# Expert results stored to their tokens' rows by indirect transfers, fetched back by nine plain ones; branches around further tiles nested

## The chip, the cores and the metric

One core of one Trainium2 chip runs the whole program. The metric is device time in microseconds (us), the median of three runs for the kernel before. The five engines (TensorE as PE, VectorE as DVE, ScalarE as ACT, GpSimd as POOL, SyncE as SP) each run their own instruction stream and meet at semaphores. SP and ACT issue plain transfers on queues q1 and q10, POOL issues its transfers, plain and indirect, on q0. All queues share the core's 16 DMA engines.

## The reference, cut to what matters

One step of a one-layer decoder: 1024 prompt tokens and 32 sample tokens, 1056 in all, width 1024, float32. First comes a mixer (gated delta net, S5), then a mixture of experts, which this change is about:

```python
x = x + mixed
# _hier_moe(h = _rmsnorm(x, norm_ffn_w)): 4 groups of 8 experts
g_sel = argmax(softmax(tok @ w_rc))               # one group
top_w, top_i = top_k(softmax(fine of that group), 2)   # two experts in it
top_w = top_w / sum(top_w) * p_sel
hu = tok @ w_eu[e]; gate, up = hu[:256], hu[256:]
act = silu(gate) * up * top_w                     # per token and expert
out = sum over the token's two experts of act @ w_ed[e]
y = _rmsnorm(x + out, norm_final_w)               # y_prompt, y_sample
```

Each token has two results, one of each of its experts; the output row is the normalised sum of its x row and the two weighted results.

## The kernel before, in words

The mixer runs to about 972 us. Then the router stage takes the nine tiles of 128 tokens (the last has 32) in the order WORD: PE multiplies a tile by w_o and by the router's weights, DVE chooses experts and works out slots (`choose`, `places`), and POOL scatters the tile's normalised rows h2 to x_d, twice, by indirect transfer (L648). x_d has 96 rows for each of the 32 experts.

The expert stage runs 32 tiles of 96 rows (one for each expert), three tiles' rows in four strips of 32, so that four strips make a chunk of 128 rows; there are 24 chunks. Per tile: PE's up product (L1289, L1292), a transposition of the next chunk (L1226), the down product of the tile before (L1261, L1265), a transposition of the activations (L1303). SP loads the weights, 2 MB and 1 MB a tile, three buffers deep (`expert`, L2720 and L2723). POOL loads the chunks of x_d (L677) into two buffers xg. ACT and DVE copy down results into one of three buffers yo (L2488, L1976), and when a chunk is complete ACT stores it with one plain transfer to y_d, in the order of slots (`chunks_done`, L2493).

If an expert has more than 96 tokens, further tiles are needed. Their number is known only at run time, so `expert_tiles` gives every engine first the 32 tiles and then six `If`s, one for each group of four further tiles. In this profile no further tile runs: the transfers of expert weights number 32, and the six `If`s are passed over on every engine. `result_rows` works out for each token and choice the row of y_d with its result (ypos_i). For the further tiles POOL also writes token numbers into idx_d (`further_rows`, inside the first `If`).

The end takes the nine token tiles in the order ORDER (the tile of 32 first). POOL gathers each tile's two sets of result rows by indirect transfer, 18 in all (L693), at most five tiles ahead. Tiles with odd p are summed on PE (L1317 adds x1 through an identity product, L1321 the two weighted results, 12 products of 512 columns a tile); those with even p on DVE (L2027, L2028 in `combine`). ACT squares and sums (L2528) and takes the root (L2530), DVE scales (L2036, L2040 in `normed`), SP stores the tile (L2780). DVE's order is combine(0), normed(0), combine(2), normed(1), normed(2), combine(4) and so on.

Eight clears of rows of y_d with zeros (L2575, Z_PARTS) lie in the projection stage of the mixer, between 313 and 456 us; ACT and POOL wait for them before they begin with experts.

Of the kernel before, what the change touches and what calls it, by code (L numbers as in the profile page):

```python
# [11 lines left out]
I32 = mybir.dt.int32  # L12
ALU = mybir.AluOpType
# [32 lines left out]
NTILE = E + TGROUP * -(-((2 * NT + E * (RT - 1)) // RT - E) // TGROUP)  # L46
NCHUNK = NTILE * RT // 128
CONV_ROWS = 4 * 12
NBK = 3
# [22 lines left out]
def hybrid_step(nc, x_p, x_s, st_conv, st_delta, st_re, st_im, norm_mix, w_in, conv_w, a_log, dt_bias, head_norm,  # L72
# [4 lines left out]
    with ctx:  # L77
# [231 lines left out]
        ypos_i = ypos_i.rearrange("p (a b) -> p a b", a=2)  # L309
        tokf, desf, tilef, idx_n, o_te = small(TT_), small(EG), small(NTILE), small(128)[0:NCHUNK], small(NOV)  # L310
        assert off[0] <= ARENA, off[0]
# [138 lines left out]
        GDEPTH = 5  # L450
        s_yg5 = s_yg + s_h2d
        GATHERED = [0, 0, 0] + [32 * ((TT_ + 1 - b) // 2) for b in range(2)]
        s_hat = sem("s_hat")
# [109 lines left out]

        def chunks_done(i):

            return [c for c in sorted({slot_of(i, s)[0] for s in range(NSTRIP)}) if chunk_last_tile(c) == i]

        heads = [slice(64 * b, 64 * b + 64) for b in range(2)]

        X_PARTS, Z_PARTS = 4, 8  # L570
        EARLY = NWE
# [4 lines left out]
        def _(pool):  # L576
# [60 lines left out]
            pl(pool.iota(des_i[:], pattern=[[1, NTILE]], base=0, channel_multiplier=0))  # L637
            pl(pool.memset(idx_n[:], 0.0))
            pool.sem_inc(s_io, 1)
            pool.wait_ge(s_yz, 1 + 16 * (X_PARTS + Z_PARTS))  # L640
            for p, i in enumerate(WORD):
                n = rows(i)
                pool.wait_ge(s_h2, p + 1)
                pool.wait_ge(s_pos, p + 1)
                if p == TT_ - 1:
                    pool.wait_ge(s_xg[0], 16)
                for j in range(2):
                    pool.indirect_dma_start(x_d, bass.IndirectOffsetOnAxis(pos_i[0:n, j, i:i + 1], 0), h2[p % 2][0:n, :],  # L648
                                            None, bounds_check=E * RT - 1, oob_is_err=False).then_inc(s_h2d[p % 2], 16)
                if p == TT_ - 2:  # L650
                    for b in range(2):
                        pool.wait_ge(s_h2d[b], 32 * ((TT_ - b) // 2))
                    pool.dma_start(xg_first, x_d[0:128, :]).then_inc(s_xg[0], 16)

            for b in range(2):
                pool.wait_ge(s_h2d[b], 32 * ((TT_ + 1 - b) // 2))

            def further_rows():
                pool.wait_ge(s_zid, 16)
                for b in range(2):  # L660
                    pool.wait_ge(s_h2s[b], H2S[b] + 16 * ((TT_ + 1 - b) // 2))
                for i in range(TT_):
                    n = rows(i)
                    for j in range(2):
                        pool.indirect_dma_start(idx_d, bass.IndirectOffsetOnAxis(ypos_i[0:n, j, i:i + 1], 0),
                                                tokf[0:n, i:i + 1], None).then_inc(s_sct, 16)
                pool.wait_ge(s_idx, 1)

            def run(lo, hi):
                if lo == E:  # L670
                    further_rows()
                for c in range(slot_of(lo, 0)[0], slot_of(hi, 0)[0]):
                    if c >= 2:
# [4 lines left out]
                    elif lo >= E:  # L678
                        pool.indirect_dma_start(xg[c % 2], None, h2_d, bass.IndirectOffsetOnAxis(idx_i[:, c:c + 1], 0)
                                                ).then_inc(s_xg[c % 2], 16)  # L680
# [5 lines left out]
            for p, i in enumerate(ORDER):  # L686
                n = rows(i)
                if p >= GDEPTH and summed_by_pe(p - GDEPTH):
                    pool.wait_ge(s_job, N_JOBS + (p - GDEPTH) // 2 + 1)
                elif p >= GDEPTH:  # L690
                    pool.wait_ge(s_acc, (p - GDEPTH) // 2 + 1)
                for j in range(2):
                    pool.indirect_dma_start(yg[2 * i + j][0:n], None, y_d,  # L693
                                            bass.IndirectOffsetOnAxis(ypos_i[0:n, j, i:i + 1], 0)
                                            ).then_inc(s_yg5[p % GDEPTH], 16)

        @block.tensor
        def _(pe):
# [571 lines left out]
            def run(lo, hi):  # L1270
                if lo == E:
                    pe.wait_ge(s_idn, 16)
                    pe.transpose(bank6()[:, 0:NCHUNK], idx_n[:], ident[0:NCHUNK, 0:NCHUNK]).then_inc(s_6, 1)
# [5 lines left out]
                for i in range(lo, hi):  # L1279
# [33 lines left out]
            for p, i in enumerate(ORDER):  # L1313
                if not summed_by_pe(p):
                    continue
                for o in range(2):
                    pe.matmul(bank_sum(p)[:, o, :], ident, x1[:, i, 512 * o:512 * o + 512], start=True, stop=False)  # L1317
                pe.wait_ge(s_yg5[p % GDEPTH], GATHERED[p % GDEPTH] + 32 * (p // GDEPTH + 1))
                for j in range(2):
# [6 lines left out]
        def _(dve):  # L1326
# [464 lines left out]
            dve.wait_ge(s_io, 1)  # L1791
            link(dve.tensor_copy(tokf, tok_i[:]))
            link(dve.tensor_copy(tilef, des_i[:]))
# [186 lines left out]
            def run(lo, hi):  # L1980
                if lo == E:
                    read6(dve.tensor_copy(idx_i[:], bank6()[:, 0:NCHUNK]))
                    dve.sem_inc(s_idx, 1)
                for c in new_chunks(lo, lo):
                    gathered(c)
                for i in range(lo, hi):
# [27 lines left out]
                    dve.wait_ge(s_hat, i + 1)  # L2014
                    dve.sem_inc(s_6f, 1)
                down(hi - 1)

# [4 lines left out]
            def combine(p):  # L2022
                i = ORDER[p]
                n = rows(i)
                dve.wait_ge(s_yg5[p % GDEPTH], GATHERED[p % GDEPTH] + 32 * (p // GDEPTH + 1))
                o = x1[0:n, i, :]
# [23 lines left out]
        def _(act):  # L2050
# [431 lines left out]
            def down(i):  # L2482
# [29 lines left out]

            act.wait_ge(s_yz, 1 + 16 * (X_PARTS + Z_PARTS))
            expert_tiles(act, run)
# [19 lines left out]
        def _(sp):  # L2534
# [69 lines left out]
            for n in range(N_JOBS_S5, N_JOBS_QKV):  # L2604
                weights(n)
                if n == AB:
                    sp.dma_start(abp[:, 0:1], a_log.rearrange("a h -> h a")).then_inc(s_abp, 16)
                    sp.dma_start(abp[:, 1:2], dt_bias.rearrange("a h -> h a")).then_inc(s_abp, 16)
                if AB < n <= AB + Z_PARTS:
                    part = (NTILE - E) * RT // Z_PARTS  # L2610
                    first = RT * E + part * (n - AB - 1)
                    cleared(y_d[first:first + part], part)
                if n == AB + 3:
# [132 lines left out]
            sp.dma_start(h2_d[128 * t:128 * t + 128, :], h2[(TT_ - 1) % 2]).then_inc(s_h2s[(TT_ - 1) % 2], 16)  # L2746
            sp.wait_ge(s_io, 1)
            sp.dma_start(idx_d.rearrange("(t p) a -> t (p a)", p=128), idx_n[:]).then_inc(s_zid, 16)
            def expert(i):
# [15 lines left out]

            def run(lo, hi):
                if lo == E:
                    sp.wait_ge(s_sct, 16 * 2 * TT_)
# [45 lines left out]
```

## Time and profile before

| | |
|---|---|
| median of three runs | 1516.19 us (1514.94 to 1517.57) |
| the profiled execution | 1514.86 us, of it 1513.1 us span |
| busy: PE, DVE, ACT, POOL | 92%, 49%, 26%, 10% of the span |
| router stage | about 972 to 1137 us |
| expert stage | about 1137 to 1442 us |
| end | about 1442 to 1513 us |
| DMA | 262.54 MB, mean 174 GB/s over the span |

Times of the trace are us from the start of the span. Each engine's line gives busy time and, ahead of an instruction, how long its engine was idle and what released it. "issue" means that the profile shows nothing that it waited for. In the view of stretches a row gives each engine's busy time with the number of instructions, then the granted TensorE clock as a share of full speed, the busy share of the DMA engines and GB/s. Instruction queues (q8, q14) are the transfers that bring the engines' own instructions.

### The profile page before, as it was taken

To read this page: it belongs to the slowest core of one execution; us is meant where nothing else is said; L and a number is where in the kernel's file an instruction comes from. 1 tells how busy PE (TensorE), PEld (TensorE's weight loads), DVE (VectorE), ACT (ScalarE), POOL (GpSimd) and SP (SyncE) were. 2 spreads that over 40 slices of the span, in tenths; PEclk is the share of its full clock that TensorE was granted. 3 is DMA by queue.
4 is the path that set the end of the run, shared out by engine and by line. 5 is a ranking of instruction groups with operands and counts; after the bars stand their busy time and mean duration, and the time that the engine had idled before them with its cause. 6 is when DMAs were issued, how large, how long until landed. Compare 5 with 4: busy or idle time off the path is not lost.

```text
span 1513.1 us, 26998 instructions
## 1 busy us (share of the span) xinstructions
PE 1386.5 (92%) x11499; PEld 967.5 (64%) x11499; DVE 743.9 (49%) x1376; ACT 389.9 (26%) x707; POOL 147.5 (10%) x152
## 2 busy tenths in 40 slices
PE   7999999999999999999967899999978999999906
PEld 6667666666666656656767666765547888888802
DVE  4667695403425532689687344355553433222324
ACT  4211100114536553232213110011112333333312
POOL 1000010000001000045036000001111000000031
PEclk9998999999999999999989899999979999999958
DMA  5243684543522113233331425334348999999755
GB/s 170 82 102 57 188 239 134 134 122 103 140 62 62 44 44 99 53 99 119 92 136 32 157 69 187 108 131 155 112 154 326 420 425 426 426 425 425 304 183 195
DMA packets 190050, 262.54 MB, mean 174 GB/s; under 512 B 61219, under 2 KB 159889, under 8 KB 181465
## 3 DMA queue, kind: packets, MB, share of 16 engines
q1 hardware_dynamic: 164668, 200.39, 39.9%
q10 hardware_dynamic: 16988, 30.29, 5.4%
q0 software_dynamic: 8256, 29.89, 5.3%
q8 instruction: 103, 1.69, 0.5%
q14 instruction: 35, 0.28, 0.1%
HBM read 184.64 MB, written 75.90 MB: 172 GB/s over the span
## 4 chain that ended last, share of the span: by engine, by line
PE 75%; DVE 9%; DMA 5%; issue 5%; ACT 3%; POOL 2%; ACTq 0%; POOLq 0%; SPq 0%; DVEq 0%
PE P L730 28%; PE P L1103 8%; PE P L1292 6%; PE P L1190 5%; PE P L1261 4%; PE P L1289 3%; DMA arena<-in_w_expert_up_dram 2%; PE P L892 2%; POOL arena L631 2%; PE P L1226 1%; PE P L1265 1%; PE P L756 1%; PE P L1147 1%; DVE arena L1601 1%; PE P L954 1%
## 5 line engine op out<-in xcount | busy, mean ns | idle before, releaser
L730 PE MATMUL P<-arena 128*128 128x352 f32 x1680 | 520.8, 465 | 4.0 <-ACT arena L2363 2.8
L730 PEld LDWEIGHTS P<-arena 128*128 128x128 f32 x1680 | 315.9, 191 | 184.5 <-issue 23.4
L1289 PE MATMUL P<-arena 128*32 128x384 f32 x1536 | 172.8, 490 | 2.3 <-DMA arena<-in_w_expert_up_dram 2.3
L1292 PE MATMUL P<-arena 128*32 128x128 f32 x1536 | 174.9, 274 | 0.0
L1292 PEld LDWEIGHTS P<-arena 128*32 128x32 f32 x1536 | 165.8, 110 | 0.3
L1103 PE MATMUL P<-arena 128*128 128x352 f32 x384 | 117.9, 468 | 3.8 <-DMA arena<-y_d 3.8
L1103 PEld LDWEIGHTS P<-arena 128*128 128x128 f32 x384 | 74.4, 194 | 45.6 <-issue 6.1
L1261 PE MATMUL P<-arena 128*32 128x512 f32 (+1 forms) x768 | 89.5, 488 | 1.5 <-DVE arena L2013 1.5
L1265 PE MATMUL P<-arena 128*32 128x256 f32 x384 | 88.7, 380 | 0.0
L1190 PE MATMUL P<-arena 128*128 128x512 f32 x192 | 87.0, 598 | 0.0
L1965 DVE COPY arena<-P 128x512 f32<-128x512 f32 x24 | 16.6, 691 | 111.2 <-PE P L1226 109.9
L1289 PEld LDWEIGHTS P<-arena 128*32 128x32 f32 x1536 | 60.6, 110 | 6.5 <-DMA arena<-in_w_expert_up_dram 3.0
L2504 ACT ACTIVATE arena<-P 32x128 f32<-32x128 f32 x96 | 26.0, 270 | 141.9 <-PE P L1292 141.1
L2488 ACT ACTIVATE arena<-P 32x768 f32<-32x768 f32 (+2 forms) x56 | 45.0, 804 | 64.1 <-PE P L1265 63.9
L1976 DVE COPY arena<-P 32x256 f32<-32x256 f32 x96 | 40.4, 421 | 42.7 <-PE P L1265 41.6
L1190 PEld LDWEIGHTS P<-arena 128*128 128x128 f32 x192 | 34.9, 190 | 36.0 <-issue 35.9
L2091 ACT ACTIVATE arena<-P 128x1056 f32<-128x1056 f32 x20 | 21.0, 1050 | 134.9 <-PE P L730 134.2
L1620 DVE SCALAR_TENSOR_TENSOR arena<-arena,par 128x1024 f32<-128x1024 f32 x36 | 46.3, 1285 | 13.6 <-ACT arena L2296 12.7
L631 POOL TENSOR_TENSOR arena<-arena,N 128x256 f32<-128x256 f32 x48 | 44.7, 931 | 76.3 <-ACT arena L2387 26.0
L1767 DVE TENSOR_TENSOR arena<-P,arena 128x352 f32<-128x352 f32 x24 | 12.6, 525 | 77.7 <-PE P L1103 77.7
L1261 PEld LDWEIGHTS P<-arena 128*32 128x32 f32 x768 | 34.9, 109 | 19.4 <-issue 3.7
L1265 PEld LDWEIGHTS P<-arena 128*32 128x32 f32 x384 | 40.3, 110 | 10.5
(420 smaller groups left out, 1854.1 us busy)
## 6 DMA issues: line engine op xcount, KB each, us to landing
arena<-in_w_expert_up_dram SPq DMA_DIRECT2D x32, 2048.0 KB, 16.6
arena<-in_w_expert_down_dram SPq DMA_DIRECT2D x32, 1024.0 KB, 11.1
arena<-in_w_in_dram SPq DMA_DIRECT2D x36, 512.0 KB, 4.2
x_d<-zero SPq DMA_DIRECT2D x4, 3072.0 KB, 21.4
arena<-x_d POOLq DMA_DIRECT2D x24, 512.0 KB, 10.7
y_d<-arena ACTq DMA_DIRECT2D x24, 512.0 KB, 9.7
y_d<-zero SPq DMA_DIRECT2D x8, 1152.0 KB, 7.8
gate_d<-arena ACTq DMA_DIRECT2D x16, 528.0 KB, 4.3
```

Of the source, the lines that this page charges most:

```text
L631: pool.tensor_tensor(ring[c % 2], src[:, :, c, :], N1[:, q, :, c].unsqueeze(2).broadcast_to([128, HP, C]), ALU.mult).then_inc(s_kb, 1)
L730: m = pe.matmul(P[:, b + j, 0:TBK], w[:, k, :], hT[:, k, TBK * j:TBK * j + TBK], start=f, stop=l)
L892: m = pe.matmul(bank[:, 0:sn * KS], wglu[:, k, 128 * j:128 * j + 128], ygT[:, k, s0:s0 + sn, :].rearrange("p a b -> p (a b)"), start=k == ...
L1103: i = pe.matmul(P[:, o, 0:TBK], w[:, k, 128 * m:128 * m + 128], v[:, k, t:t + TBK], start=k == 0, stop=k == 3)
L1190: m = pe.matmul(P[:, b + o, :], MIX[:, k, 128 * i:128 * i + 128], W_O[:, k, 512 * o:512 * o + 512], start=k == 0, stop=k == KD - 1)
L1261: m = pe.matmul(P[strip_of(slot_of(i, s)[1]), b + o, 0:n], rows_of[s][:, k, :], WD[i % NWE][:, k, 512 * o:512 * o + n], start=k == 0, stop ...
L1265: m = pe.matmul(P[strip_of(slot_of(i, NSTRIP)[1]), b + o, FF * j:FF * j + FF], rows_of[s][:, k, :], WD[i % NWE][:, k, D - FF:D], start=k = ...
L1289: m = pe.matmul(P[strip_of(s), i % 2, 0:384], rows_of[s], WU[i % NWE][:, k, 128:512], start=k == 0, stop=k == KD - 1, skip_group_check=True)
L1292: m = pe.matmul(P[RT:128, i % 2, 128 * s:128 * s + 128], rows_of[s], WU[i % NWE][:, k, 0:128], start=k == 0 and s == 0, stop=k == KD - 1, ...
L1620: link(dve.scalar_tensor_tensor(acc[:, 0:SEQ], raw[:, i:i + SEQ], wcol, acc[:, 0:SEQ], ALU.mult, ALU.add))
L1976: m = dve.tensor_copy(yo[c % 3][strip_of(slot_), D - FF:D], P[last, 2 + 2 * (i % 2) + s // 2, FF * (s % 2):FF * (s % 2) + FF])
L2488: m = act.activation(yo[c % 3][h, 0:D - FF], wide[h, 0:D - FF], ACT.Copy)
```

## The change

y_d becomes two planes of 1152 rows: plane j holds every token's result of its choice j at the token's own row. Which row a slot goes to stands in a table idx_d, by slot: it is filled with 4608 (SPARE, out of bounds, so that the row isn't stored), and for each token tile POOL scatters the numbers token and token + 1152 to the tile's slots (`slots_taken`, 18 small indirect transfers of 4 bytes a row in the router stage; the last tile's two come after the load of chunk 1). SP fills idx_d early in the router stage, and ahead of the fourth expert's weights it waits for the 18 and loads the first 24 rows of the table, which PE transposes and DVE copies as integers in the second tile. A chunk is then stored by POOL with an indirect transfer (`rows_out`), four chunks behind the loads of x_d; ACT stores nothing. Slots that hold no token aren't stored: 2112 of 3072 rows are. The clears of y_d go, with the waits for them.

After the last tile SP waits for the stores. The end's 18 gathers become nine plain transfers on SP (`rows_back`), each with both planes' rows of a token tile, five ahead; the others follow once yout(p) is ready, ahead of that tile's store. Last, the six `If`s become one `If` (any further tile) with the other five inside it.

```diff
-        y_d = dram("y_d", (NTILE * RT, D))
+        y_d = dram("y_d", (2, NTP, D))
@@ expert_tiles
-            for lo in range(E, NTILE, TGROUP):
-                with eng.If(count > lo):
-                    run(lo, lo + TGROUP)
+            with eng.If(count > E):
+                run(E, E + TGROUP)
+                for lo in range(E + TGROUP, NTILE, TGROUP):
+                    with eng.If(count > lo):
+                        run(lo, lo + TGROUP)
@@ pool
-            pool.wait_ge(s_yz, 1 + 16 * (X_PARTS + Z_PARTS))
+            pool.wait_ge(s_yz, 1 + 16 * X_PARTS)
+            def slots_taken(p):
+                i = WORD[p]
+                n = rows(i)
+                if p == 0:
+                    pool.wait_ge(s_zid, 16)
+                for j in range(2):
+                    pool.indirect_dma_start(idx_d, bass.IndirectOffsetOnAxis(pos_i[0:n, j, i:i + 1], 0), tokf[0:n, j, i:i + 1],
+                                            None, bounds_check=E * RT - 1, oob_is_err=False).then_inc(s_sct, 16)
...
+                if p < TT_ - 1:
+                    slots_taken(p)
...
+            def rows_out(c):
+                i = chunk_last_tile(c)
+                pool.wait_ge(s_idx, 1)
+                pool.wait_ge(s_yoa, i + 1)
+                pool.wait_ge(s_yov, i + 1)
+                pool.indirect_dma_start(y_d.rearrange("j t d -> (j t) d"), bass.IndirectOffsetOnAxis(idx_i[:, c:c + 1], 0),
+                                        yo[c % 3], None, bounds_check=2 * NTP - 1, oob_is_err=False
+                                        ).then_inc(s_yod[c % 3], 16)
...
+                    if c == 1:
+                        slots_taken(TT_ - 1)
+                    if c - behind >= c0:
+                        rows_out(c - behind)
+                for c in range(c1 - behind, c1):
+                    rows_out(c)
-                for b in range(3):
-                    pool.wait_ge(s_yod[b], 16 * (slot_of(hi, 0)[0] // 3))
...
-                for j in range(2):
-                    pool.indirect_dma_start(yg[2 * i + j][0:n], None, y_d, ...)
@@ pe, run
+                    if i == 1:
+                        pe.wait_ge(s_idn, 16)
+                        pe.transpose(bank6()[:, 0:NFIRST], idx_n[0:NFIRST], ident[0:NFIRST, 0:NFIRST]).then_inc(s_6, 1)
@@ act, down
-                for c in chunks_done(i):
-                    act.wait_ge(s_yoa, i + 1)
-                    act.wait_ge(s_yov, i + 1)
-                    act.dma_start(y_d[128 * c:128 * c + 128, :], yo[c % 3]).then_inc(s_yod[c % 3], 16)
@@ sp
-                if AB < n <= AB + Z_PARTS:
-                    ...
-                    cleared(y_d[first:first + part], part)
...
+                if p == 0:
+                    sp.wait_ge(s_io, 1)
+                    sp.dma_start(idx_d.rearrange("(t p) a -> t (p a)", p=128), idx_n[:]).then_inc(s_zid, 16)
...
+                if lo == 0:
+                    sp.wait_ge(s_sct, 16 * 2 * TT_)
+                    sp.dma_start(idx_n[0:NFIRST], idx_d[0:E * RT].rearrange("(t p) a -> t (p a)", p=128)).then_inc(s_idn, 16)
...
+                for b in range(3):
+                    sp.wait_ge(s_yod[b], 16 * (slot_of(hi, 0)[0] // 3))
...
+            def rows_back(p):
+                i = ORDER[p]
+                n = rows(i)
+                sp.dma_start(at(2 * i * D, 2, D)[0:n], y_d[:, 128 * i:128 * i + n, :].rearrange("j p d -> p j d")
+                             ).then_inc(s_yg5[p % GDEPTH], 16)
+            for p in range(GDEPTH):
+                rows_back(p)
             for p, i in enumerate(ORDER):
                 sp.wait_ge(s_yout, p + 1)
+                if p + GDEPTH < TT_:
+                    rows_back(p + GDEPTH)
```

The rest of the diff prepares the same for further tiles, which don't run here.

## Rows read from the trace of the kernel before

**Rows 1.** Chain that ended last, 1440 to 1480: start, us, what

```profile
1441.65 33.86 issue
1475.51 1.22 PE P L1317
```

**Rows 2.** The same chain, 1475 to the end

```profile
1492.60 11.79 DMA arena<-y_d,arena
...
1504.41 1.30 DVE arena L2027
...
1508.75 1.28 DVE arena L2040
```

**Rows 3.** Timeline of ACT, POOL and DVE: start, us, instruction, idle and releaser

```profile
1446.20 1.28 ACT L2516 ACT_TABLE_LOAD   x1 [4.56 <-issue]
...
1448.19 0.92 POOL L693 DMA_INDIRECT arena<-y_d,arena  x1 [49.53 <-issue]
...
1452.28 1.27 DVE L2027 SCALAR_TENSOR_TENSOR arena<-arena 32x1024 f32<-32x1024 f32 x1 [10.98 <-DMA arena<-y_d,arena]
```

**Rows 4.** DMA view, 1441.7 to 1475.5: queue, packets, MB, share; issues to landing

```profile
q8 instruction: 11, 0.18, 3.1%
...
y_d<-arena ACTq DMA_DIRECT2D x1, 512.0 KB, 3.5
```

**Rows 5.** The same view, 1200 to 1300

```profile
DMA packets 5431, 42.54 MB, mean 425 GB/s; under 512 B 605, under 2 KB 605, under 8 KB 2639
...
q8 instruction: 12, 0.20, 0.7%
...
arena<-in_w_expert_up_dram SPq DMA_DIRECT2D x11, 2048.0 KB, 16.1
...
arena<-x_d POOLq DMA_DIRECT2D x8, 512.0 KB, 10.7
```

**Rows 6.** PE's groups, 1200 to 1300: count, busy us, mean ns

```profile
L1289 PE MATMUL P<-arena 128*32 128x384 f32 x529 | 59.5, 488 | 0.0
```

**Rows 7.** Stretches: busy per engine, clock, DMA share, GB/s

```profile
1200.00:1300.00 100.00, 100.00 (x1538) 82.80 (x1533) 31.68 (x71) 32.01 (x72) 4.22 (x8) 1.00 1.01 425
...
1454.00:1462.00 8.00, 0.00 (x0) 0.00 (x0) 2.50 (x4) 1.44 (x3) 6.17 (x7) 0.50 0.93 307
1462.00:1468.00 6.00, 0.00 (x0) 0.00 (x0) 2.36 (x2) 0.00 (x0) 1.59 (x2) 0.50 1.00 391
1490.00:1500.00 10.00, 9.68 (x23) 4.07 (x22) 9.51 (x12) 5.71 (x12) 2.95 (x3) 1.00 1.00 361
```

**Rows 8.** Timeline of PE at the end

```profile
1478.55 2.93 PE L1317 MATMUL P<-arena,shift_id 128*128 128x512 f32 x3 [1.81 <-issue]
1481.27 4.58 PE L1321 MATMUL P<-arena 128*128 128x512 f32 x8
...
1490.83 1.88 PE L1317 MATMUL P<-arena,shift_id 128*128 128x512 f32 x4
...
1495.98 1.88 PE L1317 MATMUL P<-arena,shift_id 128*128 128x512 f32 x4
```

**Rows 9.** Waits of PE, 1160 to 1442

```profile
PE P L1289 <- DMA arena<-in_w_expert_up_dram: 2.3, 3, 0.9
```

**Rows 10.** Timeline of POOL, 1070 to 1150

```profile
1117.34 2.53 POOL L648 DMA_INDIRECT x_d<-arena  x1 [10.94 <-DVE arena L1847]
...
1125.23 0.58 POOL L653 DMA_DIRECT2D arena<-x_d  x1 [4.09 <-DMA x_d<-arena]
...
1142.81 1.14 POOL L677 DMA_DIRECT2D arena<-x_d  x2 [5.00 <-DMA x_d<-arena]
```

**Rows 11.** Timeline of PE and of SP, 1140 to 1160

```profile
1156.23 1.09 PE L1226 MATMUL P<-shift_id,arena 128*128 128x128 f32 x8
...
1146.53 0.34 SPq L2720 DMA_DIRECT2D arena<-in_w_expert_up_dram  x1
```

**Rows 12.** Timeline of PE, 955 to 1035

```profile
972.79 17.65 PE L1147 MATMUL P<-arena 128*128 128x160 f32 x128 [1.89 <-DVEq L1775]
```

More of the change, by code:

```diff
@@ L47 @@
 NCHUNK = NTILE * RT // 128
+NFIRST = E * RT // 128
+NTP = 128 * TT_
 CONV_ROWS = 4 * 12
@@ L309, in hybrid_step @@
         ypos_i = ypos_i.rearrange("p (a b) -> p a b", a=2)
-        tokf, desf, tilef, idx_n, o_te = small(TT_), small(EG), small(NTILE), small(128)[0:NCHUNK], small(NOV)
+        tokg_i = small(NCHUNK).bitcast(I32)
+        tokf, desf, tilef, idx_n, o_te = small(2, TT_), small(EG), small(NTILE), small(128)[0:NCHUNK], small(NOV)
         assert off[0] <= ARENA, off[0]
@@ L450, in hybrid_step @@
         GDEPTH = 5
-        s_yg5 = s_yg + s_h2d
-        GATHERED = [0, 0, 0] + [32 * ((TT_ + 1 - b) // 2) for b in range(2)]
+        s_yg5 = s_yg + s_xr
+        GATHERED = [0, 0, 0] + [16 + 16 * ((TT_ + 1 - b) // 2) for b in range(2)]
         s_hat = sem("s_hat")
@@ L562, in whole_rows @@
             return [(slice(a, b), c + (a < STRIP * first)) for a, b in parts]
-        def chunks_done(i):
-            return [c for c in sorted({slot_of(i, s)[0] for s in range(NSTRIP)}) if chunk_last_tile(c) == i]
         heads = [slice(64 * b, 64 * b + 64) for b in range(2)]
-        X_PARTS, Z_PARTS = 4, 8
+        X_PARTS, SPARE = 4, 4.0 * NTP
         EARLY = NWE
@@ L665, in further_rows @@
                         pool.indirect_dma_start(idx_d, bass.IndirectOffsetOnAxis(ypos_i[0:n, j, i:i + 1], 0),
-                                                tokf[0:n, i:i + 1], None).then_inc(s_sct, 16)
+                                                tokf[0:n, j, i:i + 1], None).then_inc(s_sct, 16)
+                pool.wait_ge(s_idx, 6)
+            def rows_out(c):
+                i = chunk_last_tile(c)
                 pool.wait_ge(s_idx, 1)
+                pool.wait_ge(s_yoa, i + 1)
[3 more added lines that the diff above has]
+                                        ).then_inc(s_yod[c % 3], 16)
             def run(lo, hi):
@@ L671, in run @@
                     further_rows()
-                for c in range(slot_of(lo, 0)[0], slot_of(hi, 0)[0]):
+                c0, c1 = slot_of(lo, 0)[0], slot_of(hi, 0)[0]
+                behind = min(4, c1 - c0)
+                for c in range(c0, c1):
                     if c >= 2:
@@ L678, in run @@
                     elif lo >= E:
-                        pool.indirect_dma_start(xg[c % 2], None, h2_d, bass.IndirectOffsetOnAxis(idx_i[:, c:c + 1], 0)
+                        pool.indirect_dma_start(xg[c % 2], None, h2_d, bass.IndirectOffsetOnAxis(tokg_i[:, c:c + 1], 0)
                                                 ).then_inc(s_xg[c % 2], 16)
-                for b in range(3):
-                    pool.wait_ge(s_yod[b], 16 * (slot_of(hi, 0)[0] // 3))
-            expert_tiles(pool, run)
[L686 to L691, printed above, removed]
-                for j in range(2):
-                    pool.indirect_dma_start(yg[2 * i + j][0:n], None, y_d,
-                                            bass.IndirectOffsetOnAxis(ypos_i[0:n, j, i:i + 1], 0)
-                                            ).then_inc(s_yg5[p % GDEPTH], 16)
+                    if c == 1:
[4 more added lines that the diff above has]
+                    rows_out(c)
+            expert_tiles(pool, run)
         @block.tensor
@@ L1271, in run @@
                 if lo == E:
-                    pe.wait_ge(s_idn, 16)
+                    pe.wait_ge(s_idn, 32)
                     pe.transpose(bank6()[:, 0:NCHUNK], idx_n[:], ident[0:NCHUNK, 0:NCHUNK]).then_inc(s_6, 1)
@@ L1317, in _ @@
                     pe.matmul(bank_sum(p)[:, o, :], ident, x1[:, i, 512 * o:512 * o + 512], start=True, stop=False)
-                pe.wait_ge(s_yg5[p % GDEPTH], GATHERED[p % GDEPTH] + 32 * (p // GDEPTH + 1))
+                pe.wait_ge(s_yg5[p % GDEPTH], GATHERED[p % GDEPTH] + 16 * (p // GDEPTH + 1))
                 for j in range(2):
@@ L1791, in _ @@
             dve.wait_ge(s_io, 1)
-            link(dve.tensor_copy(tokf, tok_i[:]))
+            link(dve.tensor_copy(tokf[:, 0, :], tok_i[:]))
+            link(dve.tensor_scalar(tokf[:, 1, :], tokf[:, 0, :], float(NTP), None, ALU.add))
             link(dve.tensor_copy(tilef, des_i[:]))
@@ L1981, in run @@
                 if lo == E:
-                    read6(dve.tensor_copy(idx_i[:], bank6()[:, 0:NCHUNK]))
+                    bk = bank6()[:, 0:NCHUNK]
+                    token = sc32.rearrange("p a b -> p (a b)")[:, 0:NCHUNK]
+                    dve.tensor_scalar(token, bk, float(NTP), -float(NTP), ALU.is_ge, ALU.mult).then_inc(s_idx, 1)
+                    dve.wait_ge(s_idx, 2)
+                    dve.tensor_tensor(token, token, bk, ALU.add).then_inc(s_idx, 1)
+                    dve.wait_ge(s_idx, 3)
+                    dve.tensor_scalar(token, token, float(NT - 1), None, ALU.min).then_inc(s_idx, 1)
+                    dve.wait_ge(s_idx, 4)
+                    dve.tensor_copy(tokg_i[:], token).then_inc(s_idx, 1)
+                    read6(dve.tensor_copy(idx_i[:], bk))
                     dve.sem_inc(s_idx, 1)
@@ L2015, in run @@
                     dve.sem_inc(s_6f, 1)
+                    if i == 1:
+                        read6(dve.tensor_copy(idx_i[:, 0:NFIRST], bank6()[:, 0:NFIRST]))
+                        dve.sem_inc(s_idx, 1)
                 down(hi - 1)
@@ L2024, in combine @@
                 n = rows(i)
-                dve.wait_ge(s_yg5[p % GDEPTH], GATHERED[p % GDEPTH] + 32 * (p // GDEPTH + 1))
+                dve.wait_ge(s_yg5[p % GDEPTH], GATHERED[p % GDEPTH] + 16 * (p // GDEPTH + 1))
                 o = x1[0:n, i, :]
@@ L2511, in run @@
                 down(hi - 1)
-            act.wait_ge(s_yz, 1 + 16 * (X_PARTS + Z_PARTS))
             expert_tiles(act, run)
@@ L2608, in _ @@
                     sp.dma_start(abp[:, 1:2], dt_bias.rearrange("a h -> h a")).then_inc(s_abp, 16)
-                if AB < n <= AB + Z_PARTS:
-                    part = (NTILE - E) * RT // Z_PARTS
-                    first = RT * E + part * (n - AB - 1)
-                    cleared(y_d[first:first + part], part)
                 if n == AB + 3:
@@ L2766, in run @@
             def run(lo, hi):
+                if lo == 0:
+                    sp.wait_ge(s_sct, 16 * 2 * TT_)
+                    sp.dma_start(idx_n[0:NFIRST], idx_d[0:E * RT].rearrange("(t p) a -> t (p a)", p=128)).then_inc(s_idn, 16)
                 if lo == E:
-                    sp.wait_ge(s_sct, 16 * 2 * TT_)
+                    sp.wait_ge(s_idx, 1)
+                    sp.wait_ge(s_sct, 16 * 4 * TT_)
                     sp.dma_start(idx_n[:], idx_d.rearrange("(t p) a -> t (p a)", p=128)).then_inc(s_idn, 16)
```

5 lines of the change are left out of this document (1 added, 4 removed).

## The prediction

> **What bounds the kernel now.** I first read the chain of work that ended last, in order of time, and looked for pieces without work. The largest in the last tenth is 33.86 us of "issue" on PE, from 1441.65, when ACT has copied out the last expert's result, to PE's first product of the end [rows 1]. No data is waited for there: PE's next instructions only add x1. What stands between them in the code is the wait for the two copies, the load of the count and six `If`s, passed over. The timelines of the other engines show the same six `If`s to be cheap where the groups inside them are short: ACT does its load of the count, its six and all else in 4.56 us of idle time, POOL starts its gathers at 1448.19, and DVE has its first rows at 1452.28 [rows 3]. So DMA has work from 1448 on and could feed the end, but the odd tiles wait for PE until 1475.5, and the gathers stop at five tiles ahead.
>
> Second, why PE pays 33.86 / 6 = 5.6 us for each `If`. The view of DMA shows 11 packets on the instruction queue q8 in the gap, about two for each `If` [rows 4]. In the expert stage 12 packets come in 100 us, in which PE runs 1538 products and 1533 weight loads, so about 256 instructions each [rows 5, 7]. 529 of the products are of L1289 [rows 6], which has 48 a tile, so a tile takes 100 x 48 / 529 = 9.1 us, and a group of four tiles has some 30.7 x 36.3 = 1115 PE instructions, 4.4 packets, and six groups 26. PE thus doesn't read through what it passes over; it fetches anew at each target. The Trainium skill (Runtime: NRT & Kernel Launch, Instruction fetch mechanics) says so too: prefetch is sequential, and a taken branch out of the current window must fetch its target page before it goes on. By that rule one far branch costs the same whatever it passes over, which the count of packets supports.
>
> Third, the end after 1475.5: PE, then the last gather, 11.79 us from its issue at 1492.60 to landing, then 5.65 us of DVE, ACT and DVE to 1510.03, and 3.1 us for the last store [rows 2]. Fourth, the expert stage: PE is busy 100% at clock 1.00 while DMA is busy too, at 425 GB/s [rows 5, 7]; PE's only waits for weights there are three of 2.3 us in all [rows 9]. PE sets that stage, DMA by a hair doesn't.
>
> **The change, part by part.**
>
> *Nested `If`s.* PE, ACT, DVE, POOL and SP each pass one instead of six. PE: five of six times 5.6 us go, so PE is ready at about 1441.65 + 5.6 = 1447.3; 1.8 us of fetch after the first product and 4.2 us of four products at the lower clock follow (1.22 and 2.93 us, [rows 1, 8]), and PE has x1 of its first tile in at 1453.3. What is late next is not PE but the rows.
>
> *The last store and S, the time of the first fetch.* After the last copy at 1441.65 POOL issues `rows_out(23)`, 1.0 us as its gathers take [rows 3]. Landing: the plain store took 3.5 us from its issue [rows 4], scatters to x_d 4.1 and 5.0 us after the last one's end [rows 10]; I take 3.5 after the end: 1446.2, bounds 1445.2 and 1447.7. Then SP loads the count and passes one `If`. No row shows SP's. Lower bound 0.6 (ACT's 4.56 for all seven steps), upper bound 5.6 (PE's); SP's six groups are shorter than PE's but longer than one of ACT's, so I take 3. S = 1449.3, bounds 1446 and 1453.
>
> *The end as nine plain transfers.* Bytes: tile p = 0 has 0.26 MB, the other eight 1.05 MB each, 8.65 MB; stores 4.33 MB. Rate: 361 GB/s where gathers and stores ran together, 391 after POOL had made its descriptors, 307 while it did, with DMA busy in all three [rows 7]; I take 380. The fetches of tiles 5 to 8 are issued by yout(0) to yout(3). yout(0): S + 2.0 (latency, as from the first gathers to DVE's start, [rows 3]) + 0.7 + 5.6 = S + 8.3; fetches 0 to 4, 4.46 MB, keep DMA busy until S + 12.7. yout(1): fetch 1 lands at S + 5.4; eight products 4.6 [rows 8] and 3 us of ACT and DVE: S + 13; by then DMA has work until S + 16. After that PE makes a tile in 5.15 us (1490.83 to 1495.98, [rows 8]), yout(3) comes at about S + 18.5, and DMA has work until S + 24. So DMA never runs dry, and the last fetch lands after 8.65 MB and the stores 0, 1 and 2 (1.18 MB): 9.83 / 0.38 = 25.9, + 2.0 = S + 27.9. Then 5.65 + 3.1 as before: S + 36.6 = 1486.0, against 1513.1. The step takes 27.1 us off.
>
> *Stores by POOL in the expert stage.* 24 x 1.0 us on POOL, busy 4% there [rows 7]. Each waits for the down copies of its last tile, with the next load of x_d queued behind it; by the order of loops the store of chunk c - 4 is free about 6 us before chunk c + 1 may be loaded, so it delays no load. PE, ACT and SP are not behind it. DMA: 31% of the rows aren't stored (2112 of 3072), 0.12 of 3.93 MB a tile. PE's 2.3 us of waits may go; I count 0 to -2.3, and take -1.
>
> A rule of the Trainium skill speaks against the move (SBUF — State Buffer, the box on DVE blocking SWDGE DMAs): POOL can't write descriptors while DVE runs a two-port operation. The trace has one scatter of 2.53 us [rows 10], where the first gather took 0.92 [rows 3]. By the one a store costs POOL 1.0 us, by the other 2.5, and neither is on the path but for the last, +1.5 us.
>
> *Router stage.* `slots_taken` adds 2.6 us of POOL per token tile where it stood idle 10.9 us and more [rows 10]. The last pair comes behind the load of chunk 1, so that isn't delayed, nor is PE, which needs it first; the load of chunk 2 goes out 2.6 us later, at about 1146. With 10.7 us to landing [rows 5] it lands at 1156.7, and PE transposed it at 1156.23 [rows 11]: 0 to +1.5 us, I take +0.5. SP's wait for the 18 ends near 1150; queued behind it is the fourth expert's up weight, which then stands behind 3 MB of the third's issued at 1146.5 anyway [rows 11]. PE's wait for the table in the second tile: the table lands behind those 3 MB, 7 us at 425 GB/s, near 1155, and is wanted at 1160. Its transposition and copy cost 0.3 us. SP's wait for POOL's filling at the start (about 1 us) delays loads that nobody wants before PE's 17.65 us block is over [rows 12]. If a cover is gone, these cost what is named: 2.6, 3 and 1 us.
>
> *Clears of y_d, waits of ACT.* 9.4 MB less in a stage where DMA is half idle; nothing.
>
> *Sum:* 0.5 + 0.3 - 1 - 27.1 = -27.3. From the profiled execution's 1514.86, which has 1.8 us around its span and lies 1.3 below the median: 1487.6, and by the median 1516.19 - 27.3 = 1488.9. I say 1489.
>
> **The rivals.**
>
> *PE's clock stays low.* It was 0.50, 1.2 GHz, through the idle gap [rows 7]. A product took 2.93 / 3 = 0.98 us then [rows 8]. Twelve a tile are 11.7 us against 5.15: tile 1 done at 1454.7 + 7.8, tile 7 at 1497.6, + 4.6 + 3.1 = 1505.3, so 1508. Against: PE came back to full clock within its first products at the end of the profile shown, and a slow PE would have no gaps. 7%.
>
> *The price goes by the distance passed over.* PE then starts at 1475.5 as before. yout(1) comes at 1488.8, and fetches 6, 7 and 8 with stores 1 and 2 are 4.2 MB, 11 us + 2: landed 1501.8, end 1510.5, so 1513.6. For: I don't see a branch at another distance on PE. Against: 11 packets, not 26 [rows 4]. 5%. It is also the case in which the change doesn't do what it says.
>
> *Slower: DMA becomes the bound of the expert stage.* A tile needs 3.15 + 0.39 + 0.27 = 3.81 MB in 9.1 us, 419 GB/s; with scattered rows among it the rate may fall. While POOL made descriptors it was 307, at DMA 93% busy. If only the stores' 7% run so, a tile takes 3.54 / 0.425 + 0.27 / 0.307 = 9.2 us, +3 us in all over 29 tiles. Break-even with the gain is 9.1 + 27 / 29 = 10.0 us a tile, 380 GB/s; at 361 [rows 7] each tile takes 10.55, +42: 1531. Loads of x_d would show it first, since they now share q0 with the stores. 4%.
>
> **How the numbers follow.** Forecast, with its bounds: 84%. Low: S = 1446, 410 GB/s, all waits gone: 1446 + 24.0 + 2 + 8.75 = 1480.7, 32.4 off, -2.0 for the rest, 1482. High: S = 1453 and 330 GB/s: 1453 + 29.8 + 2 + 8.75 = 1493.6, 19.5 off, and chunk 2's load and a slow last scatter, +3: 1499. The range 1482 to 1499 leaves out 16% of rivals and a little of the forecast's own tails, which makes 2 in 10. This kernel's measurement tells 0.2%, 3 us, from no change. Faster: the forecast and the clock's case, with most of what is not named, 92%. Same: mostly the distance case, 4%. Slower: 4%.
>
> **What would show it.** Right: "issue" on PE after the last expert about 6 us and two packets or so on q8; SP's first fetch near 1449 less what the stages before shift; DMA above 0.9 busy from there for some 30 us; the span's end 9 us after the last fetch lands; expert tiles still 9.1 us in the mean. Wrong: a gap of 30 us on PE; clock 0.50 beyond PE's second tile; PE idle at L1289 or L1226 for arena<-x_d in many tiles; DMA idle between fetches, which would mean that yout comes too late; SP's first fetch after 1453.

## The result and the profile after

The changed kernel takes 1488.52 us (median of four, 1487.20 to 1489.97) against 1515.57 us (median of four, 1509.96 to 1517.57) for the kernel before, 1.6% less: ratio 0.9841, 95% interval 0.9809 to 0.9872. Measured once more beside the kernel before, it was 1486.12 against 1510.46, ratio 0.9833 (0.9806 to 0.9860). The forecast was 1489.

The profiled execution took 1489.97 us, its span 1488.3 us. Of the page:

```profile
span 1488.3 us, 27022 instructions
PE 1387.0 (93%) x11500; PEld 967.7 (65%) x11500; DVE 743.6 (50%) x1378; ACT 389.9 (26%) x707; POOL 171.0 (11%) x176
DMA packets 171949, 249.03 MB, mean 167 GB/s; under 512 B 62495, under 2 KB 142757, under 8 KB 163373
arena<-in_w_expert_up_dram SPq DMA_DIRECT2D x32, 2048.0 KB, 12.9
```

PE does the same work; 13.5 MB of transfers are gone (the clears and the rows without a token). Where [rows 1] showed 33.86 us of issue, the chain now holds the last store and SP's way to the first fetch (start, us, what):

```profile
1443.95 0.77 ACT arena L2521
...
1444.83 0.50 issue
...
1445.54 4.41 DMA y_d<-arena
...
1449.96 0.02 SPq L2804
...
1450.10 0.49 SPq L541
...
1451.00 0.46 issue
1451.46 0.34 SPq L2811
...
1451.85 5.19 DMA arena<-y_d
```

The last copy ends at 1444.72, the store is out and landed at 1449.95, and SP's load of the count (L541) and its one `If` take 1.5 us. PE's timeline, against [rows 8]:

```profile
1449.38 3.78 PE L1337 MATMUL P<-arena,shift_id 128*128 128x512 f32 x4 [6.34 <-issue]
1457.08 5.82 PE L1341 MATMUL P<-arena 128*128 128x512 f32 x8 [3.92 <-DMA arena<-y_d]
1462.73 1.88 PE L1337 MATMUL P<-arena,shift_id 128*128 128x512 f32 x4
...
1475.89 3.70 PE L1341 MATMUL P<-arena 128*128 128x512 f32 x8 [0.98 <-DMA arena<-y_d]
```

PE comes 4.7 us after the last copy instead of 33.9 and now waits 3.9 us for the first rows. The last pieces of the chain answer to [rows 2]:

```profile
1471.22 8.31 DMA arena<-y_d
1479.55 1.30 DVE arena L2060
...
1483.90 1.28 DVE arena L2073
```

From the start of the first fetch (1451.46) to the last one's landing (1479.53) are 28.1 us, and 8.8 us more to the end.

### The profile page after: what moved, and what is told of

Same layout as the page of the kernel before. It is cut to its first block, busy times and chain, and to the rows that moved or that the text cites. A ratio compares the mean times of both kernels' runs of the same rounds, so it can differ in the third digit from the quotient of the medians.

```text
span 1488.3 us, 27022 instructions
## 1 busy us (share of the span) xinstructions
PE 1387.0 (93%) x11500; PEld 967.7 (65%) x11500; DVE 743.6 (50%) x1378; ACT 389.9 (26%) x707; POOL 171.0 (11%) x176
## 4 chain that ended last, share of the span: by engine, by line
PE 77%; DVE 11%; DMA 3%; ACT 3%; issue 2%; POOL 2%; ACTq 0%; SPq 0%; POOLq 0%; DVEq 0%
PE P L747 27%; PE P L1120 8%; PE P L1309 7%; PE P L1207 5%; PE P L1278 4%; PE P L1306 4%; PE P L909 2%; POOL arena L632 2%; DVE arena L1621 2%; DMA arena<-y_d 2%; PE P L1243 2%; PE P L1282 1%; PE P L1164 1%; DVE arena L1623 1%; PE P L971 1%
## 5 line engine op out<-in xcount | busy, mean ns | idle before, releaser
L2521 ACT ACTIVATE arena<-P 32x768 f32<-32x768 f32 (+2 forms) x56 | 45.0, 804 | 64.1 <-PE P L1282 63.8
L1207 PEld LDWEIGHTS P<-arena 128*128 128x128 f32 x192 | 34.9, 190 | 36.0 <-issue 35.9
L632 POOL TENSOR_TENSOR arena<-arena,N 128x256 f32<-128x256 f32 x48 | 45.0, 938 | 76.2 <-ACT arena L2420 26.5
L1278 PEld LDWEIGHTS P<-arena 128*32 128x32 f32 x768 | 34.7, 109 | 19.4 <-issue 3.7
```

The source lines that it names most:

```text
L632: pool.tensor_tensor(ring[c % 2], src[:, :, c, :], N1[:, q, :, c].unsqueeze(2).broadcast_to([128, HP, C]), ALU.mult).then_inc(s_kb, 1)
L1207: m = pe.matmul(P[:, b + o, :], MIX[:, k, 128 * i:128 * i + 128], W_O[:, k, 512 * o:512 * o + 512], start=k == 0, stop=k == KD - 1)
L1278: m = pe.matmul(P[strip_of(slot_of(i, s)[1]), b + o, 0:n], rows_of[s][:, k, :], WD[i % NWE][:, k, 512 * o:512 * o + n], start=k == 0, stop ...
L2521: m = act.activation(yo[c % 3][h, 0:D - FF], wide[h, 0:D - FF], ACT.Copy)
```

## The experiments

Every kernel below was profiled, and each span splits into the same stages. That shows where the time goes more sharply than the times do, since the mixer alone varies by 5 us from execution to execution. Stage A runs from the start of the span to PE's first product of the router stage, B from there to SP's load of the fourth expert's down weights (L2723 before, L2747 after), C from that to the fifth's, D from that to the end of the last copy (L2488, L2521), E from that to the end of the span. All are differences of times in the timelines, each good to 0.1 us; in us:

| kernel | median | A | B | C | D | E |
|---|---|---|---|---|---|---|
| before | 1515.57 | 972.8 | 187.3 | 8.3 | 273.2 | 71.5 |
| changed | 1488.52 | 972.2 | 189.7 | 12.2 | 270.7 | 43.6 |
| changed, again | 1486.12 | 969.2 | 186.8 | 12.2 | 270.7 | 44.2 |
| nested `If`s alone | 1491.81 | 970.2 | 188.9 | 8.3 | 274.2 | 50.5 |
| nested alone, again | 1490.57 | 968.3 | 188.8 | 8.3 | 273.8 | 50.3 |
| changed, `If`s flat | 1510.73 | 968.9 | 187.1 | 12.2 | 270.7 | 68.3 |
| before, short bodies on PE | 1492.75 | 972.7 | 186.7 | 8.3 | 273.2 | 52.2 |
| table in third tile | 1481.31 | 968.5 | 186.9 | 8.6 | 270.7 | 43.1 |
| the same, again | 1482.06 | 973.6 | 186.8 | 8.6 | 270.7 | 43.7 |
| the same, third time | 1482.35 | 972.2 | 188.7 | 8.6 | 270.7 | 44.3 |
| nine fetches ahead | 1485.34 | 969.9 | 189.0 | 8.6 | 270.7 | 47.0 |
| six fetches ahead | 1485.17 | 973.6 | 186.9 | 8.6 | 270.7 | 44.2 |
| every slot's row stored | 1487.04 | 970.8 | 187.1 | 8.6 | 274.4 | 43.6 |

The medians come from several chips and compare only among runs on one: nested `If`s alone, `If`s flat, short bodies and table in third tile ran on one; "changed, again", "nested alone, again", "the same, again" (table) and nine fetches ahead on another; the third run of the table in the third tile, six fetches ahead and every slot's row stored on one more. For the same code C repeats to 0.1 us, D to 0.4 and E to 1.2 (43.1 to 44.3 for the table in the third tile).

### Nested `If`s alone

```diff
 (kernel before)
-            for lo in range(E, NTILE, TGROUP):
-                with eng.If(count > lo):
-                    run(lo, lo + TGROUP)
+            with eng.If(count > E):
+                run(E, E + TGROUP)
+                for lo in range(E + TGROUP, NTILE, TGROUP):
+                    with eng.If(count > lo):
+                        run(lo, lo + TGROUP)
```

> The kernel before with the six `If`s nested and nothing else changed. Theory (the far branches of PE are the whole gain): PE's idle time behind the last expert falls from 35.5 us to about 6 us, as it did in the changed kernel (6.3), the gathers of POOL keep their form, and the end is bound by DMA: first gather near 1448, 9.83 MB at 360 GB/s, 2 us and 8.75 us, so the time is 1515.6 - 27 = 1489 us, between 1486 and 1492. Rival (the nine plain transfers gain a part of their own): gathers in the end run at 307 GB/s as in the stretch before in which POOL made descriptors, the last lands at 1482, and the time is 1493 us or more. PE's waits for expert weights (2.3 us) stay in either case, and so do the 12 us or so of the second expert tile that the changed kernel has not (it has 8.3 in the kernel before).

Measured: 1491.81 us, ratio to before 0.9857 (0.9826 to 0.9887). Its stage C is 8.3 us like before's; the 12 us are the changed kernel's alone. E falls from 71.5 to 50.5: PE starts 5.5 us after the last copy, and the 18 gathers are then what it and DVE wait for. POOL's timeline, first and last gather:

```profile
1448.66 0.92 POOL L695 DMA_INDIRECT arena<-y_d,arena  x1 [50.07 <-issue]
...
1471.88 0.94 POOL L695 DMA_INDIRECT arena<-y_d,arena  x1 [0.30 <-issue]
```

18 gathers one behind the other take 24 us on POOL, and the last then takes 11.49 us to land, while stores run too. From the start of the first gather to the last one's landing are 34.7 us at 340 GB/s (view of stretches, 1448.7 to 1483.4), against 28.1 us with plain fetches. The time is inside the theory's 1486 to 1492, at its upper end, but the kernel before takes 1513.23 us on this chip, so the gain is 21.4 us where the theory had 27. The theory thus holds for four fifths, and the rival is right that the new stores and fetches gain a part of their own: 6.1 to 6.9 us of E. Its price had been put at 4 us.

> The kernel before with nested `If`s alone, once more, to part the gain of the change. Theory (nesting is most of it, and the plain fetches gain 7 us in the end of which the table's transposition gives 3.5 back): 2 to 6 us above the changed kernel. Rival (the new stores and fetches are worth nothing): within 1 us of it.

Measured beside the changed kernel: 1490.57 against 1486.12 us, 4.5 above; their ratios to before, 0.9859 (0.9830 to 0.9887) and 0.9833 (0.9806 to 0.9860), overlap, but the four times of each do not (1489.20 to 1493.18 against 1484.65 to 1488.38). The stages say where it lies: +6.1 in E and +3.1 in D against -3.9 in C, 5.3 in sum.

> The changed kernel once more, unaltered, on the same chip as the three that follow, so that they can be compared with it. Expected near 1488 us, within 3 us; the mixer's time varies by some 2 us from execution to execution.

It came out at 1486.12.

### The `If`s flat again in the changed kernel

```diff
 (changed kernel)
-            with eng.If(count > E):
-                run(E, E + TGROUP)
-                for lo in range(E + TGROUP, NTILE, TGROUP):
-                    with eng.If(count > lo):
-                        run(lo, lo + TGROUP)
+            for lo in range(E, NTILE, TGROUP):
+                with eng.If(count > lo):
+                    run(lo, lo + TGROUP)
```

> The changed kernel with its six `If`s one behind the other again. Theory: PE idles some 34 us behind the last expert and the end starts at about 1478; nothing of the new stores and fetches can make that good, so the time is about 1513 to 1517 us, as before the change. Rival (the stores and plain fetches gain by themselves): the time is below 1505 us.

Measured: 1510.73 us, ratio 0.9989 (0.9974 to 1.0004), below the stated 1513 and no measurable gain on before. Its chain, 1430 to the end, start, us, what:

```profile
1438.91 34.71 issue
1473.62 3.78 PE P L1335 x4
```

The six `If`s take 34.7 us again, with 11 packets on q8 in them as in [rows 4]; the changed kernel's one takes 4.7 us with one packet, and a second comes by 1451. The view of DMA, this kernel from 1438.9 to 1473.5 and the changed one from 1444.8 to 1453.2:

```profile
q8 instruction: 11, 0.18, 3.5%
...
q8 instruction: 2, 0.03, 1.5%
```

Without the nesting the other edits gain 3.2 us in E, lose 3.9 in C and gain 2.5 in D.

### Short bodies for PE

```diff
 (kernel before, pe)
-            expert_tiles(pe, run)
+            def short_run(lo, hi):
+                if lo < E:
+                    run(lo, hi)
+                else:
+                    pe.wait_ge(s_te, 1)
+
+            expert_tiles(pe, short_run)
```

PE's work for further tiles is left out; with these inputs none runs.

> The kernel before with its six `If`s unchanged, but with PE's work for further tiles left out (a single wait stands in each body; no further tile runs with these inputs). It parts two causes of the 33.9 us: if PE pays for having to fetch instructions anew at a target that is far off, the six now cost about what ACT's did, 1 us each or less, with fewer than 4 packets on q8 in the gap, and the time is about 1487 to 1490 us. If each `If` costs PE 5.6 us wherever its target lies (the compare, the register, PE's queue), the gap stays at 34 us and the time at 1515 us.

Measured: 1492.75 us (two runs, 1490.58 and 1494.92), ratio 0.9872 (0.9837 to 0.9907), 3 us above the stated range, because the gathers now set the end as with nested `If`s alone: they fill the chain from 1447.78 to 1484.44. PE's timeline and its wait:

```profile
1443.45 3.78 PE L1323 MATMUL P<-arena,shift_id 128*128 128x512 f32 x4 [4.20 <-issue]
1456.48 6.45 PE L1327 MATMUL P<-arena 128*128 128x512 f32 x8 [9.25 <-DMA arena<-y_d,arena]
```

The last copy ends at 1440.93, so the load of the count and all six `If`s take 2.5 us, and no packet comes on q8. The compare and the register are thus cheap on PE; what costs is the far target. This settles the question that the price of one `If` in the changed kernel alone left open: six short ones cost 2.5 us, six long ones 34, one over all the long ones 4.4 to 6.1 (ten executions of kernels with nested `If`s, with the load of the count). The price goes by the count of far targets, not by the distance.

### The table's transposition in the third tile

The changed kernel holds a loss that the prediction had at 0.3 us. PE's timeline in its second tile:

```profile
1161.74 0.38 PE L1320 MATMUL P<-shift_id,arena 96*128 96x96 f32 x2
1164.11 0.21 PE L1325 MATMUL P<-shift_id,arena 24*128 24x24 f32 x1 [1.98 <-DVEq L2045]
1164.25 0.75 PE L1306 MATMUL P<-arena 128*32 128x384 f32 x3
```

The table uses the PSUM bank that the transposed activations have just been written to, and must wait until DVE has copied them; in that tile DVE comes late, after the mixing weights and the count of further tiles. SP's loads of down weights move apart by 3.9 us:

```profile
1161.86 0.33 SPq L2747 DMA_DIRECT2D arena<-in_w_expert_down_dram  x1
1174.02 0.33 SPq L2747 DMA_DIRECT2D arena<-in_w_expert_down_dram  x1
```

2.0 us of that is the wait. The rest goes with the clock: between these two loads 0.86 of full speed was granted (0.60 and 0.54 in the two halves of 1164 to 1168, just behind the wait, 1.00 from 1168), in the like stretch of before 1.00. The changed kernel's second profile shows 0.86 again.

```profile
1161.90:1174.00 12.10, 10.12 (x136) 8.43 (x136) 3.42 (x11) 1.86 (x5) 0.00 (x0) 0.86 1.02 395
```

```diff
 (changed kernel; PE, in run)
                     m.then_inc(s_up, 1)
+                    if i == 2:
+                        pe.wait_ge(s_idn, 16)
+                        pe.transpose(bank6()[:, 0:NFIRST], idx_n[0:NFIRST], ident[0:NFIRST, 0:NFIRST]).then_inc(s_6, 1)
...
-                    if i == 1:
-                        pe.wait_ge(s_idn, 16)
-                        pe.transpose(...)
 (DVE: its copy moves from the end of i == 1 to the start of i == 2)
```

> The changed kernel with the transposition of the table moved from behind the second tile's last product, where PE stood idle 2.0 us for DVE and then ran at half clock, to behind the third tile's up product, where its bank has long been free. Theory: SP's weights of the fourth and fifth expert go out 8.3 us apart again instead of 12.2, and the time falls by 3 to 4 us against the changed kernel, to about 1485 us. Rival: DVE's late work in the second tile (mixing weights and the number of further tiles) makes the loss, not the transposition; then it stays, and the time is 1488 us.

Measured: 1481.31 us, ratio 0.9799 (0.9774 to 0.9824). C is 8.6 us, 3.6 less, at clock 1.00, so the rival fails: DVE's late work is unchanged and the loss is gone. The time is 7 below the changed kernel's first median, more than C explains.

> The changed kernel with the table's transposition in the third tile, once more. By the gap of SP's loads of weights (12.1 us in the changed kernel, 8.6 in this one) it should stand 3 to 4 us below the changed kernel; in the first look it stood 7 below it on another chip. If it is 3 to 4 here, the rest of that difference was the chip and the mixer; if it is 7, something else gained too.

Beside the changed kernel on one chip: 1482.06 against 1486.12, 4.1 us below, of which C is 3.6. The other 3 us of the first comparison were the chip and the mixer (A and B).

> The same with five fetches ahead, on the same chip, for the comparison: an end of 43 to 44 us and a time near 1482 us.

1482.35 us, ratio 0.9797 (0.9768 to 0.9826). All three ratios of this kernel lie between 0.9796 and 0.9799, and it is the fastest of those tried: 1481.31 us beside 1513.23 for the kernel before on the same chip, 31.9 us less.

### Nine and six fetches ahead

```diff
 (kernel with the table in the third tile)
-        s_yg5 = s_yg + s_xr
-        GATHERED = [0, 0, 0] + [16 + 16 * ((TT_ + 1 - b) // 2) for b in range(2)]
+        s_yg5 = s_yg + s_xr + s_tb
+        GDEPTH = 9
+        GATHERED = [0, 0, 0] + [16 + 16 * ((TT_ + 1 - b) // 2) for b in range(2)] + [128] * 4
```

> The same with the end's nine fetches issued at once, each on a semaphore of its own, instead of five ahead. Theory (the end is bound by DMA, 12.98 MB of fetches and stores at about 0.38 MB a us): the last fetch lands earlier, at S + 2 + 8.65 / 0.38 = S + 25 instead of S + 28, but the stores then stand behind it and the last one ends at S + 2 + 34 or so, so only 0 to 2 us are gained against the run before. Rival (the last tile's chain from its fetch is the bound and DMA has room): the full 3 us are gained.

Measured: 1485.34 us, 3.3 above the kernel with five ahead on the same chip; E is 47.0 instead of 43.7. Both theories failed. DVE's waits in the end name what neither had:

```profile
DVE arena L2061 <- DMA arena<-y_d: 11.0, 1, 11.0
DVE arena L2074 <- DMA out_dram<-arena: 4.5, 1, 4.5
```

The first store, 0.13 MB, stands behind all nine fetches on SP's queue and takes 15.30 us to land, now a piece of the chain that ended last:

```profile
1454.40 15.30 DMA out_dram<-arena
```

There are four output buffers, so yout(4) must wait for it.

With `GDEPTH = 6` (one more semaphore):

> The kernel with the table's transposition in the third tile and six fetches ahead instead of five. In the changed kernel's end DMA moves 287 GB/s for 3 us while it waits for the fetch that yout(1) issues, between stretches at 389 and 390. Theory (the end is bound by DMA and this dip is the only loss): the dip goes and the end, from the last copy to the span's end, takes 42 to 43 us instead of 43.1 to 44.2; the time falls by about 1 us, which is less than the times can show. Rival (as with nine ahead, stores stand behind fetches and DVE waits for a free output buffer): the end grows, towards the 47.0 us with nine ahead.

Measured: 1485.17 us, ratio 0.9805 (0.9779 to 0.9832), beside 1482.35 and 0.9797 for five ahead; E is 44.2 against 44.3, but E also holds the way to the first fetch, which varies. From the first fetch to the end of the span it is 37.5 us, where the six profiles with nested `If`s and five ahead have 35.9 to 36.9, so nothing was gained. The dip went (399 and 418 GB/s where 389 and 287 stood), and DVE waited 2.0 us for an output buffer in its place. The chain that ended last now runs through a store, no longer through the last fetch:

```profile
1462.78 11.20 DMA out_dram<-arena
```

The theory that the dip is the only loss fails; the rival's mechanism is there, but small.

### Every slot's row stored

```diff
 (kernel with the table in the third tile)
-NTP = 128 * TT_
+NTP = 128 * TT_ + E * RT
...
-            pl(pool.memset(idx_n[:], SPARE))
+            pl(pool.iota(idx_n[:].bitcast(I32), pattern=[[1, 128]], base=128 * TT_, channel_multiplier=128))
+            pl(pool.tensor_copy(idx_n[:], idx_n[:].bitcast(I32)))
```

> The kernel with the table's transposition in the third tile, but every slot's row is stored: the 960 slots without a token go to rows of their own behind the tokens' rows, so that POOL's stores move 12.6 MB again instead of 8.7. It parts two causes of the faster expert stage (270.7 us from SP's fourth down weight to the last copy, against 273.2 to 274.1 in kernels that store slot by slot). Theory (fewer bytes): PE's waits for expert weights come back, 2 us or more, the stretch takes 273 us or more, and the landing of the up weights goes from 12.9 back to 16 us. Rival (the queue: POOL's queue carries loads and stores one behind the other, so that the weights' queue has a half of the turns instead of a third): the stretch stays at 270.7 and PE doesn't wait.

Measured: 1487.04 us, ratio 0.9839 (0.9811 to 0.9867), beside 0.9797 for the kernel that it was made from. D, which begins at the fifth expert's down weights (the expectation calls them the fourth), is 274.4 instead of 270.7 us, and PE waits again:

```profile
PE P L1307 <- DMA arena<-in_w_expert_up_dram: 3.3, 3, 1.5
```

None of the eight profiles of kernels that store only the tokens' rows has such a wait. So it is the bytes that take PE's waits away, not the queue. The landing of the up weights isn't shown for this kernel, so that part of the expectation stays open; in two profiles of the kernel that it was made from it is 13.0 and 15.9 us in the stretch 1200 to 1300, and PE waits in neither, which makes the landing a poor sign of the wait.

## Why the prediction was right

*What bounds the kernel.* Right, and shown by four kernels (before, flat again, nested alone, short bodies): far targets, 5.6 to 5.8 us each on PE with about two packets each. The packets decided rightly between the price by count and that by distance.

*PE ready.* 1447.3 was 5.65 us after the last copy; measured 4.7, and 4.4 to 6.1 over all profiles with nested `If`s. PE then waits for rows, as said.

*The last store and S.* In the changed kernel S is 6.7 us after the last copy, against 7.6 predicted. Two errors cancel in part: the store, issued 0.8 us after the copy, lands 5.2 us after it (4.5 stated), but SP's load and `If` take 1.5 us, not 3. Over eight profiles of the changed kernel and those made from it with nested `If`s, S is 6.4 to 8.3 us after the last copy.

*The nine fetches.* S + 28.1 against S + 27.9, and 8.8 us after it against 8.75. The mean rate to the last landing, 9.83 / 26.1 = 0.377 MB a us, is the one taken, but by luck. DMA did run nearly dry, which the prediction excluded. The view of stretches of the changed kernel:

```profile
1452.50:1465.00 12.50, 8.58 (x15) 3.49 (x15) 7.09 (x8) 3.47 (x7) 0.00 (x0) 0.65 1.00 389
1465.00:1468.00 3.00, 3.00 (x9) 1.33 (x8) 2.96 (x4) 0.71 (x3) 0.00 (x0) 1.00 0.95 287
1468.00:1479.50 11.50, 10.52 (x25) 4.17 (x23) 9.86 (x12) 5.71 (x12) 0.00 (x0) 1.00 1.00 390
```

The rate is higher than 380 outside the dip. Within it, fetch 6 waits for yout(1) and went out at S + 14.5 instead of S + 13: PE's first eight products took 5.8 us, still partly at the lower clock, not 4.6. And the prediction set the issue of that fetch against the end of DMA's work (S + 16), though it counts 2 us from an issue to the first rows elsewhere: the rate was 98 and 74 GB/s in the two halves of 1467 to 1468 and 270 in the us after, 2 to 3 us behind the issue at 1465.92. Step and rate were each off by a little, in opposite directions, and that they met at S + 28 is luck; the six-ahead run shows that going one fetch deeper does not win the dip back.

*The form of the fetches and of the nesting.* The prediction made one step of both. They part into 21 us of E for the nesting and 6.1 to 6.9 for the rest; as no run has the plain fetches without the new stores, that these 6 to 7 us are the fetches' is read from the gathers' 24 us on POOL and not shown alone.

*Stores by POOL.* -1 us predicted, -2.5 measured (D), the low end of the stated 0 to -2.3 and a little beyond; the bytes are the cause, as said. POOL's stores took 0.97 to 1.02 us each, so the Trainium skill's rule on DVE and the descriptors (SBUF — State Buffer, the box on DVE blocking DMA) didn't bite in this stage: the 2.5 us that the prediction set beside it isn't seen in any of the 24. Whether DVE ran a two-port operation beside any of them, no run here shows.

*Router stage.* The load of chunk 2 cost nothing: PE isn't shown waiting for it. The table's 0.3 us is the step that failed: it cost 3.9 us. The prediction looked at when the table's data lands, which was in time, and not at the bank in which it is transposed, which DVE had yet to empty.

*Rivals.* The clock was 0.50 from 1450 to 1460, 0.86 from there to 1465 and full from then on; PE's second tile, from 1462.73, already runs at the full rate (1.88 us for four products). The low-clock case thus cost 1.2 us of its 19. The distance case is refuted by the changed kernel's own gap and by the short bodies. DMA wasn't the bound of the expert stage at 418 GB/s (1200 to 1300); with all rows stored, at 426, it held the stage up by 3.7 us, so the margin seen in the prediction is real and as thin as it said.

In sum: C +3.9, D -2.5, E -27.9, together -26.5 for a forecast of -27.3. The mechanism was right, and so is most of the sum, which E makes up; that the whole came out so near is in part luck, since C lost 3.1 us more than the 0.8 stated for it, against 1.5 more gained in D and 0.8 in E, and since the medians differ by 27.0 us here and by 24.3 where both kernels were measured again.

## What to carry to other kernels

Idle time with nothing awaited, ahead of the first instruction behind runtime branches, is worth a look at the instruction queues: a handful of 16 KB packets there means that each passed-over body costs a fetch, and one outer branch around rare work pays for it once. When a small step borrows a bank or buffer, ask who empties it and how late that engine is in just that iteration; moving the step by one tile took back 3.6 of the 3.9 us that it cost. Where DMA bounds a stretch, more fetches ahead only push stores behind them, and a small ring of output buffers turns that into a wait.

## What the runs showed of the hardware

A far branch cost PE 5.7 us with about two instruction packets; a near one at most 0.4 us (2.5 us for six and the load of the count). On the same engine, with the same compare, six near ones are thus all but free. The Trainium skill (Runtime: NRT & Kernel Launch, Instruction fetch mechanics) says that a taken branch whose target lies outside two pages of instructions waits for a fetch of the target's page; the 34.7 us with 11 packets for six long bodies, and 2.5 us with none for six short ones, agree.

18 indirect gathers (16 of 128 rows of 4 KB, two of 32 rows) took POOL 24 us to issue one behind the other, 1.33 us each; nine plain transfers of the same bytes took SP 0.34 to 0.47 us each.
